# A hybrid attention and MoE layer on one core: projections, head norms and merge projections put in another order

## The reference, cut to what matters

```python
h = rms_norm(x, g_attn); proj = h @ w_in                     # x: 256 x 1024, w_in: 1024 x 4896
q_n, kv_n, gate_n, qkv_f, f_logit, merge_logit = split(proj)
k_c, v_c = rms_norm(compress(kv_n[0])), compress(kv_n[1])    # blocks of 32 tokens, a small MLP (w_ck1, w_cv1)
o_nsa = gates * (compressed + selected + window attention)   # 8 heads of 64
o_fox = forgetting_attention(rms_norm(q_f), rms_norm(k_f), v_f, cumsum(log_sigmoid(f_logit)))
merge = sigmoid(merge_logit + b_merge)                       # 2 x 1024 channels
y = merge[0] * (o_nsa @ w_up_nsa) + merge[1] * (o_fox @ w_up_fox)
x = x + y @ w_out
x = x + moe_ffn(rms_norm(x, g_mlp))                          # top 4 of 32 experts, each 3 x 1024 x 1024, float32
```

## Time and profile before

| | us |
|---|---|
| median of 3 runs | 1210.77 (1210.0 to 1216.22) |
| the profiled execution's own time | 1214.83 |
| span of its profile | 1213.1 |
| start to the end of project 0 | 30.4 |
| to the end of project 5 | 64.7 |
| to the end of project 11 | 106.5 |
| first attention map's scores | 129.6 |
| first expert load issued | 227.3 |

### The profile page before, as it was taken

The page is one execution under the profiler, slowest core; times in us unless marked ns, Lnnn a source line. Parts: engine busy times, 40 slices in busy tenths (PEclk is TensorE's granted clock), DMA queues, the critical chain, the costliest instruction groups (busy, mean ns, idle before and its releaser), DMA issues.

```text
span 1213.1 us, 14640 instructions
## 1 busy us (share of the span) xinstructions
PE 1120.7 (92%) x5782; PEld 540.8 (45%) x5782; DVE 437.1 (36%) x891; ACT 175.6 (14%) x363; POOL 127.1 (10%) x120
## 2 busy tenths in 40 slices
PE   3998999999999999999999999999999999899997
PEld 3777799885333433333333333333333333333332
DVE  3665566683323332233232222222222222222222
ACT  3453354432000000000000000000000000000000
POOL 4462443550000000000000000000000000000000
PEclk9898899999989999999999999999999999999999
DMA  8852223289999999999999999999999999999995
GB/s 258 262 207 70 71 73 133 78 346 364 428 386 428 427 427 427 430 427 430 427 429 428 428 430 428 430 427 429 429 428 429 428 430 427 429 429 428 429 428 230
DMA packets 49422, 438.80 MB, mean 362 GB/s; under 512 B 6538, under 2 KB 13774, under 8 KB 24814
## 3 DMA queue, kind: packets, MB, share of 16 engines
q1 hardware_dynamic: 47748, 437.97, 86.8%
q10 hardware_dynamic: 1642, 0.39, 0.2%
HBM read 437.30 MB, written 1.05 MB: 361 GB/s over the span
## 4 chain that ended last, share of the span: by engine, by line
PE 50%; DMA 41%; DVE 6%; issue 1%; POOL 1%; ACT 1%; SPq 1%; DVEq 0%; ACTq 0%
PE bank L1539 28%; DMA ring<-in_w_e_up_dram 20%; DMA ring<-in_w_e_gate_dram 20%; PE bank L1523 3%; PE bank L1553 2%; DVE w_lo L364 2%; PE bank L1535 1%; PE bank L1394 1%; PE bank L1396 1%; PE bank L1395 1%; PE bank L1573 1%; PE bank L1363 1%; POOL small L563 1%; PE bank L1249 1%; PE bank L1424 1%
## 5 line engine op out<-in xcount | busy, mean ns | idle before, releaser
L1539 PE MATMUL bank<-ring,hT 128*64 128x512 f32 x2048 | 466.9, 598 | 20.2 <-DMA ring<-in_w_e_gate_dram 19.4
L1539 PEld LDWEIGHTS bank<-ring,hT 128*64 128x64 f32 x2048 | 137.7, 136 | 302.4 <-issue 256.8
L1539 PE MATMUL bank<-ring,heads 128*64 128x512 f32 x1024 | 228.9, 600 | 0.4 <-DVE heads L1165 0.4
L1198 DVE TENSOR_TENSOR x<-x,bank 128x512 f32<-128x512 f32 x128 | 82.3, 684 | 143.5 <-PE bank L1553 143.5
L1147 DVE TENSOR_SCALAR heads<-bank 128x512 f32<-128x512 f32 x32 | 22.1, 692 | 307.9 <-PE bank L1539 307.9
L1539 PEld LDWEIGHTS bank<-ring,heads 128*64 128x64 f32 x1024 | 71.1, 138 | 136.9 <-issue 129.4
L364 POOL TENSOR_TENSOR w_lo<-ring,w_hi 128x512 fp32r<-128x512 f32 (+2 forms) x61 | 105.6, 1749 | 100.1 <-ACT w_hi L615 100.1
L743 ACT ACTIVATE work<-bank 128x256 f32<-128x256 f32 x32 | 12.3, 383 | 502.1 <-PE bank L1566 502.1
L1553 PE MATMUL bank<-heads,work 64*128 64x512 f32 x256 | 72.8, 641 | 1.5 <-ACT heads L748 0.8
L615 ACT ACTIVATE w_hi<-ring 128x512 fp32r<-128x512 f32 (+2 forms) x88 | 61.6, 724 | 28.9 <-PE bank L1258 17.3
L1523 PE MATMUL bank<-work,xn 128*128 128x128 f32 x528 | 64.5, 275 | 0.0
(11 more groups left out here) (276 smaller groups left out, 1069.0 us busy)
## 6 DMA issues: line engine op xcount, KB each, us to landing
ring<-in_w_e_gate_dram SPq DMA_DIRECT2D x64, 2048.0 KB, 33.6
ring<-in_w_e_up_dram SPq DMA_DIRECT2D x64, 2048.0 KB, 35.2
ring<-in_w_e_down_dram SPq DMA_DIRECT2D x64, 2048.0 KB, 34.8
ring<-in_w_in_dram SPq DMA_DIRECT2D x8, 2048.0 KB, 8.6
ring<-in_w_out_dram SPq DMA_DIRECT2D x2, 2048.0 KB, 8.5
ring<-in_w_in_dram SPq DMA_DIRECT2D x2, 1024.0 KB, 10.2
ring<-in_w_ck_dram SPq DMA_DIRECT2D x1, 2048.0 KB, 8.4
heads<-in_w_cv_dram SPq DMA_DIRECT2D x1, 2048.0 KB, 14.0
```

What stands on the lines that cost most here:

```text
L1198: ins = nc.vector.tensor_tensor(x[:, t, 512 * h:512 * h + 512], x[:, t, 512 * h:512 * h + 512], bank67[:, j % 2, :], ALU.add)
L1539: last = mm(bank[C * half:C * half + C, :], lhs(kk), w[:, k, 512 * half:512 * half + 512], start=(kk == 0 and m == "down"), stop=(kk == KD ...
```

## The change

It regroups the work ahead of and within the attention maps. All products stay as they were; ten matmuls of constants are new.

```diff
# SP, ACT: order of the loads
-            load("kv", BLOCKS[0][1][:1])
             sp.wait_ge(vrow_set, 1)
+            sp.dma_start(vrow[R_GA:R_GA + 8, :], a["g_attn"][0]...).then_inc(gain_rows_in, 16)
+            sp.dma_start(view["kv"][:, 0:4, :], w_in[:, 0:4, C_KV:C_KV + 512]).then_inc(kv_lead_in, 16)
+            sp.dma_start(view["kv"][:, 4:8, :], w_in[:, 4:8, C_KV:C_KV + 512]).then_inc(ring_in[...], 16)
+            load("kw", BLOCKS[1][1])
+            # then the five brow rows (before: on ACT's queue), then vrow; w_c2, w_r, gain_m behind cv1 (load_late)
...
# POOL: the two inverts of x's norm ahead of spread, own_head, blk and the token columns
+            for t in range(NT):
+                invert()
             step(nc.gpsimd.memset(spread[:, :], 0.0))
...
# which low parts DVE makes: in blocks 1 to 5 slice 6 too
-        LOW_BY_VECTOR = [OUT + 3, OUT + 5, OUT + 7]
+        LOW_BY_VECTOR = [j for j in range(N_SPLIT) if j % 2 or (j >= KD and j % KD == 6)] + [OUT + 3, OUT + 5, OUT + 7]
# ACT: order of the first copies
+            keep_high_lead(0)
+            keep_high_tile(0, 0)
+            keep_high_lead(1)
+            keep_high_tile(0, 1)
+            ... # slices 2 to 5, tile (1, 0), slice 6, tile (1, 1), slice 7
# DVE: head_norm cut in head_mean (up to mean_made) and head_scale (waits inv_made), work between
-                head_norm(t, 256, G, ks_tok[:, t, :, 0:DH])
+            head_mean(0, G)
+            keep_low_chunks(1, (1,))
+            head_scale(0, 256, G, ks_tok[:, 0, :, 0:DH])
+            keep_low_chunks(1, (3, 5, 6, 7))
...
+            head_mean(3, G)
+            make_blocks(0)
+            head_scale(3, 0, G, kw_tok[:, 1, :, 0:DH])
+            make_blocks(1)
...
+            keep_low_chunks(4, (5, 6, 7))
+            head_mean(7, HF)
             dve.wait_ge(hid_tanh, 1)
             nc.vector.scalar_tensor_tensor(out=hflat, ...).then_inc(hid_made, 1)
+            head_scale(7, 0, HF, fk_tok[:, 1, :, 0:DH])
...
+            keep_low_chunks(5, (6, 7))
+            head_mean(9, HF)
+            dve.wait_ge(inv_made, n_inv[0] - 1)
             ... # ck65, vc16 -> ck_kept
+            head_scale(9, 0, HF, fq_tok[:, 1, :, 0:DH])
# PE: start
             pe.wait_ge(consts_made, 1)
-            pe.wait_ge(vec_in, 16 * 13)
-            nc.tensor.transpose(TB[0][:, 0:R_ALL], vrow[:, :], ...).then_inc(vec_turned, 1)
+            for _ in range(10):
+                mm(OB[0][:, 0:P], ident[:, :], ident[:, :], start=True, stop=True)
+            pe.wait_ge(gain_rows_in, 16)
+            nc.tensor.transpose(TB[0][:, 0:KD], vrow[0:KD, :], ...).then_inc(gain_turned, 1)
...
             project(0, "kv", 512)
+            pe.wait_ge(vec_in, 16 * 12)
+            pe.wait_ge(gain_kept, 1)
+            nc.tensor.transpose(TB[0][:, 0:R_ALL], vrow[:, :], ...).then_inc(vec_turned, 1)
...
             project(4, "q", 512)
+            project(5, "q", 512)
             pe.wait_ge(blk_made, 2)
             ... # compression, first layer
-            project(5, "q", 512)
# merges
-        MERGE_AT = {m: i for i, m in enumerate(m for m in range(24) if m % 3 != 2)}
+        EARLY = 4
+        MERGE_AT = {m: EARLY + i for i, m in enumerate(range(0, 24, 2))}
...
+            merge(0)
+            turn_heads(6)
+            turn_heads(7)
+            merge(1)
             pe.wait_ge(cp_made, 1)
             ... # turn cp
+            turn_heads(8)
+            turn_heads(9)
+            merge(2)
+            turn_heads(10)
+            turn_heads(11)
+            merge(3)
+            turn_heads(12)
+            turn_heads(13)
# ACT in that stretch (before: units 0 to 12, cp's exp after unit 4, a keep_high after units 6, 8, 10)
+            keep_high(MERGE)
+            for i, u in enumerate((0, 2, 4)):
+                keep_unit_a(u)
+                if i < 2:
+                    keep_high(MERGE + 1 + i)
+            act.wait_ge(cs_max, 1)
+            nc.scalar.activation(cp, cp, ACT.Exp).then_inc(cs_exp, 1)
+            keep_high(MERGE + 3)
+            for c in range(EARLY):
+                keep_merge(c)
+                keep_unit_a(6 + 2 * c)
+                if c < EARLY - 1:
+                    keep_high(MERGE + 4 + c)
```

More of the change, by code:

```diff
@@ L290, in build @@
         BLOCKS = [
-            ("kv", [(w_in[:, :, C_KV + c:C_KV + c + 256], c, 256) for c in (0, 256)], 8, 512),
+            ("kv", in_cols(C_KV, 512), 8, 512),
             ("kw", in_cols(C_KW, 280) + [(w_in[:, :, C_FL:C_FL + 8], 280, 8)], 8, 288),
@@ L454, in _ @@
                         sp.wait_ge(*user)
-                if i:
+                if name not in ("kv", "kw"):
                     load(name, pieces)
+                if name == "cv1":
+                    load_late()
                 if name == "fk":
@@ L694, in _ @@
                     c = MERGE_AT[m]
-                    act.wait_ge(merge_done, c + 1)
-                    nc.scalar.activation(mergeT[:, c, :], PJ[c % 2][:, 0:T], ACT.Tanh, scale=0.5,
-                                         bias=scaled[:, c:c + 1]).then_inc(merge_made, 1)
+                    keep_merge(c)
                     keep_high(MERGE + c + 3)
@@ L800, in _, with keep_low_tile, keep_low_chunks @@
                 norm_row_tile(t, xn_made)
+            dve.wait_ge(gain_turned, 1)
+            nc.vector.tensor_copy(vcol[:, R_GA:R_GA + KD], TB[0][:, 0:KD]).then_inc(gain_kept, 1)
+            dve.wait_ge(gain_kept, 1)
+            keep_hT_tile(R_GA, [PJ[0], PJ[1], S[0], S[1]], 0, 0)
+            def keep_low_tile(t):
+                q = slice(P * t, P * t + P)
+                for j in range(2):
+                    ks = slice(4 * j, 4 * j + 4)
+                    dve.wait_ge(hT_made, 2 * t + j + 1)
+                    dve.wait_ge(hT_hi_made, 2 * t + j + 1)
+                    nc.vector.tensor_tensor(hT_lo[:, ks, q], hT[:, ks, q], hT_hi[:, ks, q], ALU.subtract).then_inc(hT_lo_made, 1)
+            def keep_low_chunks(b, chunks=(1, 3, 5, 7)):
+                for k in chunks:
+                    keep_low(dve, nc.vector, KD * b + k, lo_made_v)
+            keep_low_tile(0)
+            keep_hT_tile(R_GA, [PJ[0], PJ[1], S[0], S[1]], 0, 1)
+            keep_low_chunks(0)
+            keep_low_tile(1)
             dve.wait_ge(vec_turned, 1)
-            step(nc.vector.tensor_copy(vcol[:, :], TB[0][:, 0:R_ALL]))
+            step(nc.vector.tensor_copy(vcol[:, KD:R_ALL], TB[0][:, KD:R_ALL]))
             nc.vector.tensor_scalar(scaled[:, 0:16], vcol[:, R_BM:R_BM + 16], 0.5, None, ALU.mult)
@@ L1341, in _, with merge @@
             last.then_inc(cs_done, 1)
-            for u in range(6, len(UNITS)):
-                turn_heads(u)
+            def merge(c):
+                if c >= 2:
+                    pe.wait_ge(merge_made, c - 1)
+                else:
+                    pe.wait_ge(proj_read_a, 11 + c)
+                pe.wait_ge(*low_done(MERGE + c + 1))
+                w = quarter(MERGE + c)
+                for k in range(KD):
+                    mm(PJ[c % 2][:, 0:T], w_hi[:, k, w], hT_hi[:, k, :], start=(k == 0), stop=False)
+                    mm(PJ[c % 2][:, 0:T], w_hi[:, k, w], hT_lo[:, k, :], start=False, stop=False)
+                    last = mm(PJ[c % 2][:, 0:T], w_lo[:, k, w], hT_hi[:, k, :], start=False, stop=(k == KD - 1))
+                last.then_inc(merge_done, 1)
+            merge(0)
+            turn_heads(6)
+            turn_heads(7)
+            merge(1)
             pe.wait_ge(cp_made, 1)
@@ L1386, in values @@
                     last.then_inc(o_done, 1)
-            def merge(c):
-                if c >= 2:
-                    pe.wait_ge(merge_made, c - 1)
-                pe.wait_ge(*low_done(MERGE + c + 1))
-                w = quarter(MERGE + c)
-                for k in range(KD):
-                    mm(PJ[c % 2][:, 0:T], w_hi[:, k, w], hT_hi[:, k, :], start=(k == 0), stop=False)
-                    mm(PJ[c % 2][:, 0:T], w_hi[:, k, w], hT_lo[:, k, :], start=False, stop=False)
-                    last = mm(PJ[c % 2][:, 0:T], w_lo[:, k, w], hT_hi[:, k, :], start=False, stop=(k == KD - 1))
-                last.then_inc(merge_done, 1)
             pe.wait_ge(kept_a, 7)
             pe.wait_ge(kept_v, 7)
-            pe.wait_ge(proj_read_a, 12)
             def turn_outputs(mix):
```

206 lines of the change are left out of this document (105 added, 101 removed).

## The result

The changed kernel takes 1194.64 us in the median of 4 runs (1193.38 to 1196.62), the kernel before 1213.49 in the same session (four runs, 1210.0 to 1216.44). The ratio is 0.9846, interval 0.9815 to 0.9876: 18.9 us faster. The forecast was 1183.5 with a range of 1176 to 1193. The direction is right, the time lies 11.1 us above the forecast and outside the range, and the gain is 8.4 us smaller than the 27.3 forecast. The profiled execution took 1193.38.

The account below looks back on a forecast made before the run. An expert-load stream keeping the DMAs full bounds the end; PE's chain before it sets its start. 10.5 + 9.0 + 7.8 = 27.3 us off 1214.83 gives 1187.5, less 4.1 to the median: 1183.5, range 1176 to 1193.

Parts of the forecast that it names:

- The thesis: Before the last map: each us cut from PE's chain before 216 us moves the whole expert-load stream forward by one us.
- Rival E: Expert loads: loads, not PE's chain, set the front, so time stays within 6 us of 1210.8; chance 0.03.
- Part 1: Start: earlier norms and kv loads let project 1 begin at 19.9 instead of 30.43; 10.5 us less.
- Rival A: Start: bound by its loads, so it gives 4 to 6 us instead of 10.5, total 1189; chance 0.17.
- Part 2: Projections: compression behind project 5 wins 4.7 us and closed gaps 4.3; together 9.0 us less.
- Nearly all of the 6.5 us lies at 1.2 GHz: Compression's 128 matmuls: mostly run at the low clock, so estimated at 3.5 us at full clock.
- the 4.7: Projections: with project 5 ahead of the compression, project 6 begins 4.7 us earlier.
- all three go: Projections: the gaps of 0.98, 1.31 and 2.00 us, ending with late DVE work, all close; 4.3 us less.
- Part 3: Heads and maps: twelve maps with merges instead of sixteen win 11.5 us, heads pay 4.2; 7.8 us less in all.
- I count on the merges keeping it at 2.4 GHz.: Heads: four merges moved there keep PE's clock up, where about half the stage ran at 1.2 GHz.
- the 30 that the prediction had named as a sign of being wrong: Heads: the prediction is wrong if this stage takes over 30 us; it forecast 27.3 from project 11's end.
- Rival B: Heads: PE falls to 1.2 GHz while turning units and merges begin slow; merge gain about 0, total 1191; chance 0.15.

Follow-up runs that it names:

- busy_o: Changed kernel with five constant matmuls in each of the two 1.3 us waits for branch outputs in the maps; 1192.38 us, ratio 0.9836.
- again: The changed kernel run once more, unchanged, for more executions and a second profile; 1194.44 us, ratio 0.9843.
- merge_first: Changed kernel with merge 0 ahead of the compressed scores and merge 2 right behind merge 1; 1193.72 us, ratio 0.9847.
- best: Changed kernel with the edits of merge_first and busy_o, and ACT emptying units 0, 2, 4 before each w_hi quarter; 1190.47 us, ratio 0.9817.
- hid_between: Changed kernel with the compression's first layer put back between projects 4 and 5; 1196.58 us, ratio 0.9866.
- joined5: Changed kernel with the five norms of token tile 0 no longer split; 1196.61 us, ratio 0.9869.
- joined_tail: Changed kernel with the earlier kernel's DVE and POOL order for norms 7, 8, 9 and the compressed keys; 1197.27 us, ratio 0.9868.
- no_warm: Changed kernel without the ten constant matmuls at the start; 1192.83 us, ratio 0.9837.
- delay: Changed kernel with 44 constant matmuls added behind project 11; 1204.48 us, ratio 0.9926.

## Why the prediction was wrong

**The thesis was right.** PE's chain before the last map sets the stream: 44 matmuls, 9.8 us, in that chain moved the end by 10, and over fourteen profiles the span follows the first expert load with a slope of 0.92. Rival E is out.

**Part 1, the start: right in its end, unsure in its size.** Project 1 at 20.1 to 20.4 in all changed profiles, forecast 19.9. ACT's first copy of kv begins at 9.72 (forecast 9), DVE's last hT_lo is what project 1 waits for, as forecast. Rival A did not happen. But 30.43 belongs to that one execution; in two other profiles of the same start project 1 begins at 28.36 and 27.82, so the part is worth 7.4 to 10.3 us.

**Part 2, the projections: right in kind, the 9.0 was 7.8 in the pair read and about 5 against the other two profiles of that stretch (74.86 and 74.85 us, changed kernels 68.3 to 70.8).** The wait ahead of project 5 is 1.19 us (forecast 1.3) and the compression 3.6 us (3.5). Two steps failed. "Nearly all of the 6.5 us lies at 1.2 GHz" was true of the execution read, but the compression took 5.3 and 3.6 us in the two others, with the same wait of 2.9 ahead of it: that part of the 4.7 is a chance of the clock, not a property of the order. And "all three go" did not hold. Of the gaps of 0.98, 1.31 and 2.00 us only the second one went. Ahead of project 11 PE still waits 0.85 us in every profile that keeps the late norms split. Ahead of hid's turn the pair read has no wait, but it is the exception: in the eight other profiles that keep the compression behind project 5 and the late norms split PE waits 1.17 to 1.61 us for DVE there, more than the 0.98 before. Why the read execution has none is open. The 4.3 forecast for the three gaps were 3.5 in the pair and about 2 otherwise (project 6 to the end of project 11: 41.8 us before, 38.35 in the pair, 39.6 to 40.0 in the others). In the working, the terms listed for head_scale(3) add up to 51.6 and not 51.0, unless the power runs beside the blocks; and the 0.43 and 0.28 us are durations of rows of two matmuls, not of one.

**Part 3, the merges: the step of the mechanism that failed.** "I count on the merges keeping it at 2.4 GHz." They don't. Merge 0 itself took 5.03 us (98.01 to 103.04) instead of 3.06, the compressed scores 4.67 to 6.85 instead of 3.5, and in the maps a fall of 7 us behind a wait of 1.3 us costs 3.1 us, one of 4 us 1.6 (77.68 and 79.28 against busy_o's 74.58). In the pair the clock cost 3.0 us from the scores to the end of merge 0; the heads are still only 1.1 over the forecast, since the scores began 0.4 earlier than summed up and the pieces behind merge 0 took 14.1 us instead of 15.5. That is luck: two errors met. So the heads lost 5.3 (8.5 in again) instead of 4.2, and the maps gave 8.7 to 10.3 instead of 12.0; without the falls they would have given 13.4. In again the heads took 31.63 us, over the 30 that the prediction had named as a sign of being wrong. The step between two scores did behave: 4.53 us with a merge, 1.65 without, as in the earlier trace rows. Net 5.0, by stages and by medians, against 7.8. Rival B named this mechanism; it put part 3 at about 0, which is 5 too low, since the merges that follow the first one run at full clock. merge_first, with the same instructions in another order, has merge 0 at 2.95 us and no fall there; in best, with that order too, merge 0 is fast and a fall of 3 to 4 us comes behind the scores. So the order decides which work pays; that it does away with the fall is not shown.

**The base.** The forecast took 4.1 us off because the profiled execution lay above a median of three runs. The later sessions' medians of before are 1212.4 to 1214.3, so 0.5 to 2.4 us was the right step down. From 1183.5 to the 1194.64 measured it is thus: 4.5 of mis-sized terms (0.5 for the start, 1.2 for the projections, 1.1 for the heads, 1.7 for the maps), 1.4 in the expert stage of that profile, 4.1 of base, and 1.3 by which the changed kernel's median lies above its profiled execution; together 11.3, with rounding. The last two terms, 5.4 us, are about half of the miss and lie in which executions were taken for the base and for the profile.

**Which part failed most.** In the pair it is part 3, 2.8 of the 4.5. By medians it is not: of the 19.9 us between again and its kernel before part 3 has 5.0 (forecast 7.8), and parts 1 and 2 have 14.9 (forecast 19.5), 4.6 short. The profile that the forecast was worked out from was a slow execution in just these parts (project 1 at 30.43, compression 6.5 us), and what it had at 1.2 GHz was counted as won.

**What stays open.** The intervals are some 2 to 4 us wide to each side, so the single steps of 1 to 3 us (hid_between, joined5, joined_tail, busy_o, merge_first) rest on the traces, not on the times. Why the same wait is followed by a fall in one execution and not in the next was not settled.

## What to carry to other kernels

Where a saturated stream at the end is started by a compute chain, count the chain alone and test it by delaying it once; here every us there was worth 0.9 to 1. Read two profiles of the kernel before, and charge a stretch's clock as a chance and not as a property, since one execution can hold 10 us more at 1.2 GHz than the next. Dense work moved into a thin stretch did not hold the clock up there: what stood right behind the thin part ran slow. Put ahead of it, it ran fast itself. Short waits between small matmuls are worth filling with constant ones: it cleared the falls in all four places tried.

## What the runs showed of the hardware that was not expected

- A wait of only 1.3 us in the maps, between small matmuls, was followed by 7 us at 1.2 GHz (154 to 161 us, granted clock 0.52), and the dense merge that begins at 155.8 inside it ran slow until 160.6. Twelve of eighteen such waits were followed by a fall, none of the four that were filled.
- PE can be busy for all of a stretch and yet run at 1.2 GHz: 8.00 of 8.00 us busy at 0.50 between 95 and 103 in again, nearly all of it 16-column scores. Waits of 1.33 and 0.43 us among the transposes stand ahead of the fall, so that thin work alone brings it about is not shown.
- In the first microseconds the granted clock is not to be trusted: the earlier trace rows give 1.00 for the start of the kernel before, and no_warm has 1.00 over the 3.69 us of its transposes, whose pitch is 0.23 us, while the 88 records of delay's 44 constant matmuls took 9.99 us, 0.11 each, at 2.4 GHz. There the pitch tells the clock.
- Two executions of one kernel on the same operands differ by 6 us in when the expert loads start (204.54 and 210.47).
